# One-core two-block transformer kernel: first norm's gain spread by TensorE, two weight chunks in halves, two key chunks and VectorE's contexts moved

## What is computed

```python
def first_block(x, mem, ...):                       # DEPTH = 2
    mem_n = rmsnorm(mem, mem_norm_gain)
    for l in range(DEPTH):
        h = rmsnorm(x, g[0])
        y = even_mixer(h, ...) if l % 2 == 0 else odd_mixer(h, ...)   # recurrence+pooling | band attention
        x = x + rmsnorm(y, g[1])
        h = rmsnorm(x, g[2])
        x = x + rmsnorm(memory_cross_attention(h, mem_n, w_mem_q[l], w_mem_kv[l], w_mem_o[l]), g[3])
        h = rmsnorm(x, g[4])
        x = x + rmsnorm(squared_relu_mlp(h, w_ff1[l], w_ff2[l]), g[5])
# second block: SwiGLU, stick-breaking attention (layer 0) or sliding window with sinks (layer 1), SwiGLU
```

## Time and profile before

| | |
|---|---|
| median of 3 runs | 1888.31 us |
| profiled execution | 1888.25 us, span 1886.5 us |
| mean granted TensorE clock | 0.994 |
| TensorE busy (matmul) | 1838.3 us, 97% of the span |
| VectorE, ScalarE, GpSimd busy | 54%, 45%, 4% |
| DMA | 318.51 MB, mean 169 GB/s |
| chain that ended last | TensorE 93%, VectorE 3%, ScalarE 2% |

### The profile page before, as it was taken

The page is one execution under the profiler, slowest core; times in us unless marked ns, Lnnn a source line. Parts: engine busy times, 40 slices in busy tenths (PEclk is TensorE's granted clock), DMA queues, the critical chain, the costliest instruction groups (busy, mean ns, idle before and its releaser), DMA issues.

```text
span 1886.5 us, 30104 instructions
## 1 busy us (share of the span) xinstructions
PE 1838.3 (97%) x12718; PEld 1675.1 (89%) x12718; DVE 1022.3 (54%) x1041; ACT 855.2 (45%) x1040; POOL 71.2 (4%) x117
## 2 busy tenths in 40 slices
PE   7999999999999999999999999999999999899998
PEld 6989979999989889998999897899989998779997
DVE  5665454446456464446555544655565555765554
ACT  5535454446555445445333454433343334453333
POOL 1000000000120000000000011000010000110000
PEclk9999999999999999999999999999999999899999
DMA  8616345556556355555555544455555554336552
GB/s 278 205 31 220 129 154 181 186 193 198 162 163 202 104 174 192 185 178 168 181 191 184 161 134 135 148 187 180 193 176 181 192 183 156 112 98 205 187 178 89
DMA packets 224428, 318.51 MB, mean 169 GB/s; under 512 B 5568, under 2 KB 194128, under 8 KB 224352
## 3 DMA queue, kind: packets, MB, share of 16 engines
q1 hardware_dynamic: 219552, 301.48, 48.6%
q0 software_dynamic: 4800, 15.94, 2.7%
HBM read 316.35 MB, written 1.05 MB: 168 GB/s over the span
## 4 chain that ended last, share of the span: by engine, by line
PE 93%; DVE 3%; ACT 2%; issue 1%; DMA 1%; POOL 0%; SPq 0%; DVEq 0%; ACTq 0%
PE C L1429 49%; PE Y L1441 29%; PE Y L1429 7%; DVE xn L1002 1%; ACT xn L631 1%; PE C L1797 1%; PE C L1655 1%; DMA raw<-in_w_in_ab 1%; PE C L1563 1%; PE C L1602 1%; PE Y L1776 1%; PE Y L1610 1%; PE C L1590 0%; PE Y L1580 0%; PE Y L1489 0%
## 5 line engine op out<-in xcount | busy, mean ns | idle before, releaser
L973 DVE TENSOR_TENSOR w_lo<-raw,w_hi 128x2048 fp32r<-128x2048 f32 x284 | 649.5, 2290 | 498.6 <-ACT w_hi L626 498.3
L626 ACT ACTIVATE w_hi<-raw 128x2048 fp32r<-128x2048 f32 x284 | 542.5, 1910 | 371.6 <-PE Y L1441 219.6
L1429 PE MATMUL C<-at_h,w_hi 128*128 128x256 f32 x2160 | 592.0, 284 | 2.6 <-ACT at_h L655 2.6
L1429 PE MATMUL C<-at_h,w_lo 128*128 128x256 f32 x2160 | 590.7, 283 | 0.0
L1429 PE MATMUL C<-at_l,w_hi 128*128 128x256 f32 x2160 | 590.4, 283 | 0.0
L1429 PEld LDWEIGHTS C<-at_h,w_hi 128*128 128x128 f32 x2160 | 405.2, 192 | 7.2 <-issue 4.6
L1429 PEld LDWEIGHTS C<-at_l,w_hi 128*128 128x128 f32 x2160 | 405.3, 192 | 3.0 <-issue 0.5
L1429 PEld LDWEIGHTS C<-at_h,w_lo 128*128 128x128 f32 x2160 | 405.3, 192 | 0.0
L1441 PE MATMUL Y<-w_hi,hid_h 128*128 128x512 f32 x656 | 205.0, 394 | 6.9 <-issue 6.9
L1441 PE MATMUL Y<-w_lo,hid_h 128*128 128x512 f32 x656 | 203.4, 391 | 0.0
L1441 PE MATMUL Y<-w_hi,hid_l 128*128 128x512 f32 x656 | 203.4, 391 | 0.0
(11 more groups left out here) (249 smaller groups left out, 2199.9 us busy)
## 6 DMA issues: line engine op xcount, KB each, us to landing
raw<-in_ffn_w_in SPq DMA_DIRECT2D x88, 1024.0 KB, 5.0
raw<-in_w_ff SPq DMA_DIRECT2D x64, 1024.0 KB, 5.2
raw<-in_ffn_w_out SPq DMA_DIRECT2D x44, 1024.0 KB, 5.0
raw<-in_w_mem_kv SPq DMA_DIRECT2D x16, 1024.0 KB, 5.9
raw<-in_w_qkv SPq DMA_DIRECT2D x12, 1024.0 KB, 5.3
raw<-in_sb_w_qkv SPq DMA_DIRECT2D x12, 1024.0 KB, 5.1
raw<-in_w_in_ab SPq DMA_DIRECT2D x10, 1024.0 KB, 7.9
raw<-in_w_mem_q SPq DMA_DIRECT2D x8, 1024.0 KB, 5.1
```

What stands on the lines that cost most here:

```text
L626: nc.scalar.activation(w_hi[:, n % RING, :], raw[:, n % RAW, :], ACT.Copy).then_inc(hi_split, 1)
L973: V.tensor_tensor(w_lo[:, n % RING, :], raw[:, n % RAW, :], w_hi[:, n % RING, :].bitcast(f32), ALU.subtract).then_inc(lo_split, 1)
L1429: last = mm(to, *passes[k][j], start=step == 0, stop=step == 3 * KT - 1)
```

## The change

Start: the first gain arrives as one row in `first_row`; TensorE spreads it over 128 partitions by two f32 matmuls with a row of ones (`first_ones`, set by GpSimd) into Y banks 0 and 1, ahead of the 20 warm-ups, and VectorE scales from there. The first two weight chunks (`HALVED` = 2) are loaded, split and used in halves of four k-tiles, in an order written out on each engine; the first chunk's result goes to Y bank 2. GpSimd waits until both front halves are rounded before it issues the second gain and all later transfers. Two of layer 1's four key chunks run after the memory attention of layer 0, in a "meanwhile" stage that takes the place of its ("post",) and ("norm", "at"); there the norm's transposes come after both chunks and `clear_y` after the first feed-forward chunk. In layer 1's stage two key chunks are left. In `att` VectorE does the contexts ahead of shares or keeps.

```diff
-                net += [("meanwhile", mem_k(1), mem_k_to), ("att", "band", qkv_cols, "w_o_att"),
+                net += [("meanwhile", mem_k(1)[2:], mem_k_to[2:]), ("att", "band", qkv_cols, "w_o_att"),
...
-            net += [("cols", mem_q(l), q_to), ("softmax", 4), ("rows", "w_mem_o", l),
-                    ("post",), ("norm", "at"), ("relu_ff", l)]
+            net += [("cols", mem_q(l), q_to), ("softmax", 4), ("rows", "w_mem_o", l)]
+            net += [("meanwhile", mem_k(1)[:2], mem_k_to[:2])] if l == 0 else [("post",), ("norm", "at")]
+            net += [("relu_ff", l)]
...
+            def load_halves(src, n):
+
+                to = raw[:, n, :].rearrange("p (k n) -> p k n", k=KT)
+                sp.dma_start(to[:, 0:4, :], src[:, 0:4, :]).then_inc(front_in[n], 16)
+                sp.dma_start(to[:, 4:8, :], src[:, 4:8, :]).then_inc(loaded[n], 16)
+
+            sp.dma_start(first_row, gain_rows[0][None, :]).then_inc(first_gain_in, 16)
             for b in range(TB):
                 sp.dma_start(x[:, b, :], a["x"][0, b * P:(b + 1) * P, :]).then_inc(tokens_in[b], 16)
-            sp.dma_start(gain[:, 0, :], gain_rows[0].partition_broadcast(P)).then_inc(first_gain_in, 16)
...
+            nc.gpsimd.memset(first_ones, 1.0).then_inc(first_ones_set, 1)
             pool.dma_start(ident[:], a["ident"]).then_inc(ident_in, 16)
...
+                if s[0] == "even_cols":
+                    pool.wait_ge(front_hi, HALVED)
...
-                    hi(0)
-                norm_hi(to, at, C)
-                if at.chunk == 0:
-                    for n in range(1, AHEAD):
-                        hi(n)
+                    hi_front(0)
+                    norm_hi(to, at, C, [0])
+                    hi_back(0)
+                    norm_hi(to, at, C, [1])
+                    hi_front(1)
+                    hi_back(1)
...
+                    lo_front(0)
+                    norm_lo(to, at, C, [0])
+                    lo_back(0)
+                    norm_lo(to, at, C, [1])
+                    lo_front(1)
+                    lo_back(1)
...
+                    for k in CONTEXTS_BEHIND.get(j - 1, ()):
+                        contexts(k, at, kind)
                     if p is not None:
                         if kind == "band":
                             shares("band", p, at)
                         else:
                             keeps(p)
-                    for k in CONTEXTS_BEHIND.get(j - 1, ()):
-                        contexts(k, at, kind)
...
+            def col_halves(n, bank, split=None):
+
+
+                wh, wl = (w[:, n, :].rearrange("p (k c) -> p k c", k=KT) for w in (w_hi, w_lo))
+                for i in range(2):
+                    part = slice(i * P, (i + 1) * P)
+                    for step, (half, j) in enumerate(((0, 0), (0, 1), (0, 2), (1, 0), (1, 2), (1, 1))):
...
+                if same:
+                    pe.wait_ge(cols_copied, at.copied)
                 col_chunk(n, "T", at_h, at_l, C[:, 0, :], split=at.turned - 4)
+                if same:
+                    clear_y(at)
...
+                        pe.wait_ge(cols_copied, at.copied + 1)
                         norm(at, Y)
...
+                        pe.wait_ge(first_ones_set, 1)
+                        pe.wait_ge(first_gain_in, 16)
+                        for k in range(2):
+                            gained = mm(Y[:, k, :], first_ones, first_row[:, k * 512:(k + 1) * 512], start=True, stop=True)
+                        gained.then_inc(first_gain_ready, 1)
                         stay_warm(WARM_START)
```

More of the change, by code:

```diff
@@ L231, in build @@
         at_lo = sem("at_lo")
-        first_gain_in = sem("first_gain_in")
+        first_gain_in, first_ones_set, first_gain_ready = sem("first_gain_in"), sem("first_ones_set"), sem("first_gain_ready")
+        front_in = [sem(f"front_in{i}") for i in range(HALVED)]
+        front_hi, front_lo = sem("front_hi"), sem("front_lo")
         gains_in = [sem(f"gains_in{i}") for i in range(2)]
@@ L626, in hi, with hi_front, hi_back @@
                 nc.scalar.activation(w_hi[:, n % RING, :], raw[:, n % RAW, :], ACT.Copy).then_inc(hi_split, 1)
+            def hi_front(n):
+                act.wait_ge(front_in[n], 16)
+                nc.scalar.activation(w_hi[:, n, 0:1024], raw[:, n, 0:1024], ACT.Copy).then_inc(front_hi, 1)
+            def hi_back(n):
+                act.wait_ge(loaded[n], 16)
+                nc.scalar.activation(w_hi[:, n, 1024:2048], raw[:, n, 1024:2048], ACT.Copy).then_inc(hi_split, 1)
             def guess(src, b, at):
@@ L648, in norm_guess, with norm_hi @@
                     guess(mem_x[:, b, :] if to == "mem" else x[:, b, :], b, at)
-            def norm_hi(to, at, banks):
-                for b in range(TB):
+            def norm_hi(to, at, banks, blocks=range(TB)):
+                for b in blocks:
                     for h in range(2):
@@ L687, in copied @@
                 f = ACT.Silu if specs is even_cols and i < 2 else ACT.Copy
-                nc.scalar.activation(to[i], tiles(C[:, i % 4, :], 2), f).then_inc(cols_copied, 1)
+                src = Y[:, 2, :] if specs is even_cols and i == 0 else C[:, i % 4, :]
+                nc.scalar.activation(to[i], tiles(src, 2), f).then_inc(cols_copied, 1)
             def part_copied(i, kind, at):
@@ L700, in meanwhile @@
                 post(at, behind_rows)
-                for i in range(len(specs)):
+                n = len(specs)
+                for i in range(n):
                     hi(at.chunk + i + AHEAD)
-                    if i == len(specs) - 1:
+                    if n > 2 and i == n - 1:
                         norm_hi("at", then, Y)
@@ L707, in meanwhile @@
                         norm_guess("at", then)
+                if n == 2:
+                    norm_hi("at", then, Y)
             def cols(specs, to, at):
@@ L974, in lo, with lo_front, lo_back @@
                                 ALU.subtract).then_inc(lo_split, 1)
+            def lo_front(n):
+                dve.wait_ge(front_hi, n + 1)
+                V.tensor_tensor(w_lo[:, n, 0:1024], raw[:, n, 0:1024], w_hi[:, n, 0:1024].bitcast(f32),
+                                ALU.subtract).then_inc(front_lo, 1)
+            def lo_back(n):
+                dve.wait_ge(hi_split, n + 1)
+                V.tensor_tensor(w_lo[:, n, 1024:2048], raw[:, n, 1024:2048], w_hi[:, n, 1024:2048].bitcast(f32),
+                                ALU.subtract).then_inc(lo_split, 1)
             def newton(guess, mean, scratch):
@@ L998, in scaled @@
                 if at.norm == 0:
-                    dve.wait_ge(first_gain_in, 16)
-                else:
-                    dve.wait_ge(gains_in[at.norm % 2], 16 * ((at.norm + 1) // 2))
+                    dve.wait_ge(first_gain_ready, 1)
+                    return V.scalar_tensor_tensor(xn[:, b, :], src, stat[:, 6, j:j + 1], Y[:, 0:2, :].rearrange(flat), ALU.mult, ALU.mult)
+                dve.wait_ge(gains_in[at.norm % 2], 16 * ((at.norm + 1) // 2))
                 return V.scalar_tensor_tensor(xn[:, b, :], src, stat[:, 6, j:j + 1], gain[:, at.norm % 2, :], ALU.mult, ALU.mult)
@@ L1007, in norm_scale, with norm_lo @@
                     scaled(src, b, at, to == "same").then_inc(xn_ready, 1)
-            def norm_lo(to, at, banks):
+            def norm_lo(to, at, banks, blocks=range(TB)):
                 h, l = (mem_h, mem_l) if to == "mem" else (at_h, at_l)
-                for b in range(TB):
+                for b in blocks:
                     for k in range(2):
@@ L1023, in norm @@
                 if at.chunk == 0:
[L1024 to L1029, removed]
+                    lo_front(0)
[4 more added lines that the diff above has]
+                    lo_back(1)
+                else:
+                    norm_lo(to, at, C)
+                if to == "same":
+                    rope_keys(at)
+                elif at.chunk > 0:
                     lo(at.chunk - 1 + AHEAD)
-                else:
-                    rope_keys(at)
             def post(at, behind_lo=False):
@@ L1430, in col_chunk @@
                 last.then_inc(chunk_done, 1)
+            def col_halves(n, bank, split=None):
[3 more added lines that the diff above has]
+                    for step, (half, j) in enumerate(((0, 0), (0, 1), (0, 2), (1, 0), (1, 2), (1, 1))):
+                        ready = (((front_hi, n + 1), (front_lo, n + 1)), ((hi_split, n + 1), (lo_split, n + 1)))[half][j == 1]
+                        pe.wait_ge(*ready)
+                        if split is not None:
+                            pe.wait_ge(at_lo if j == 2 else at_hi, split + 2 * i + half + 1)
+                        for k in range(4 * half, 4 * half + 4):
+                            still, moving = ((at_h, wh), (at_h, wl), (at_l, wh))[j]
+                            last = mm(bank[:, i * S:(i + 1) * S], still[:, k, part], moving[:, k, :],
+                                      start=step == 0 and k == 0, stop=step == 5 and k == KT - 1)
```

(14 more changed lines are left out.)

9 lines of the change are left out of this document (8 added, 1 removed).

## The result

The changed kernel takes 1877.52 us (median of 4 runs, 1875.51 to 1879.12) against 1888.3 us: ratio 0.9942, 95% interval 0.9925 to 0.9959, so 10.8 us faster, where 15.9 were forecast (1872.4). The mean granted clock rose from 0.994 to 0.996.

The account below looks back on a forecast made before the run. TensorE was taken as the bound, so only its idle or slow-clock stretches could be won. Start -5.2, key chunks -3.6 and VectorE's order -7.1 made -15.9, so 1872.4 us; range 1869.0 to 1879.5.

Parts of the forecast that it names:

- The start: From launch to the end of chunk 1: first chunk at 15.5, chunk 1 done by 27.0, gain 5.2 us.
- The pair: Two f32 gain matmuls ahead of the warm-ups on TensorE's queue: 1.0 to 2.0 us, taken as 1.9.
- The 20 warm-ups: On TensorE behind the gain matmuls: 1.0 us still slow, 3.85 fast, the clock rising 2.9 us after 6.16 again.
- Rival 2: Start gains 0 to 2.6: one-row matmuls don't wake the clock, warm-ups stay slow, or halves late; 1875 to 1878; chance 0.11.
- GpSimd held back: GpSimd waits until about 17.6; VectorE's bounds at 27.1 at worst, chunk 3's split 29.4, wanted 32.8: hidden, 3.4 us spare.
- Key chunks: Two key chunks moved to layer 0: +5.5 us there, -9.1 in layer 1, together -3.6.
- VectorE's order: Contexts first in both attentions: stands shrink by 1.2 and 2.2 us, clock held at both; together -7.1.
- term of 1.84 us for each kept clock: At each attention's shortened stand the clock holds, saving 1.84 us in the row chunk behind; ends 0 and -1.84.
- Rival 3: The attention stands are not the low part's, as the profile names "issue": -7.1 goes, 1879.5; chance 0.04.
- rival 1: Clock falls in the two norm stretches (+3.7) or at the band attention (+1.8): 1874 to 1878; chance 0.24.
- rival 4: TensorE stays at half clock through chunks 0 to 3, costing 23 us: 1895; chance 0.02.
- Rival 5: At the start the first block's data and warm-ups run closer, 1 to 3 us more: 1869 to 1871; chance 0.08.

Follow-up runs that it names:

- e6: Changed kernel with 20 warm-ups first, then the pair of one-row matmuls, then the wait for the identity: 1873.28 us.
- e11: Changed kernel with five more one-row f32 matmuls in place of the 20 warm-ups: 1880.64 us.
- e1: Kernel before with only the change's start (gain spread by TensorE, two chunks in halves, GpSimd held back): 1885.95 us.
- e2: Kernel before with only the two key chunks moved: 1885.74 us.
- e5: Changed kernel with the pair of one-row matmuls ahead of TensorE's wait for the identity, warm-ups still behind it: 1873.39 us.
- e8: Changed kernel without GpSimd's wait for the two front halves: 1877.34 us.
- e4: Changed kernel without one-row matmuls, the first gain coming as a broadcast transfer behind x: 1873.76 us.
- e3: Kernel before with only VectorE's contexts moved ahead of shares and keeps: 1881.63 us.
- e7: Changed kernel with the norm's low parts ahead of the last weight chunk's in the stages of two key chunks: 1874.65 us.
- e12: e10 without GpSimd's wait for the two front halves: 1869.8 us.
- e10: Changed kernel with e7's edit, the gain by a broadcast transfer behind x, and 28 warm-ups ahead of the wait for the identity: 1867.54 us.
- e9: Changed kernel with e7's edit; at the start 14 warm-ups, the one-row pair, 6 warm-ups, then the wait for the identity: 1869.47 us.

## Why the prediction was right, and where it was not

**The start: right in sign, mis-sized by 4.1 us.** Chunk 0 was put at 15.5 and came at 19.64. Three terms make that up.
- The pair: 1.9 us forecast, 3.77 measured. The step that failed is the reading of the earlier trace rows. Its "x4" was taken for four matmuls at 0.49 us; they are two, with two records each. So a pair costs 1.97 at the full clock, as there and as in e6 (1.92), and 3.77 at half. That is 1.9 us.
- The 20 warm-ups: 4.85 us forecast, 6.92 measured. The step that failed is "the clock rises 2.9 us after 6.16 again". It took the pair for work that brings the rise nearer; e11 shows that it does not, and that is 1.0 of the 2.1 (the 20 alone took 5.83). And it took one execution's 2.9 us for a property. In the profiles, from the first warm-up to the change of spacing, it was 2.8 (before), 3.3 (e1), 3.4 (e2), 3.8 (e5), 4.7 (e6, e8), 5.1 (the changed kernel), 5.5 (e4), 5.8 (e3), 5.9 us (e7); in the later ones 2.5 (e12), 3.3 (e10) and over 5 (e9). That is the other 1.1.
- The identity came at 6.54, not 6.16 (0.4); transposes and three warm-ups took 0.2 less.

Rival 2 had the mechanism as its first condition ("the two one-row matmuls do not wake the clock") and its times, 1875 to 1878, hold the result; with 0.11 it had too little. Its third condition, late halves, is not what happened.

A step that the prediction didn't take is the question why the start should wait for TensorE at all. It said that the warm-ups, not the gain, set the transposes, and then weighed only the cost of putting more in front of them. The warm-ups need zeros, not the identity; e6, e9 and e10 start them at 1.44.

**The spread.** The forecast treated the start as one number. Before, the first chunk hung on the weight transfer, and it stood at 19.01, 19.20 and 19.01 in the kernel before, e2 and e3, with rises 2.8, 3.4 and 5.8 us after the warm-ups began. In the changed kernel it hangs on the warm-ups, so each microsecond of a later rise costs half a microsecond. The times of the runs do not settle whether this shows: four of the changed kernel lie within 3.6 us, four of before beside them within 0.9, but 21 of before in a later series within 3.5. The start is not the only place that differs between executions: a clock that falls behind a stand costs 1.5 us in e4's profile and 2.6 in e2's.

**GpSimd held back: right that nothing waits.** VectorE's wait for the bounds ended at 32.01 (forecast 27.1 at worst), since they were issued at 22.5 and not 17.6; the split behind them ended at 34.9 and TensorE wanted it at 36.9. Hidden, with 2 us to spare. That the wait itself buys nothing (e8) the forecast left open.

**Key chunks: right to 0.1 us.** Feed-forward 14.66 us behind the rows' end (14.65), projections 9.0 us earlier (9.1), with VectorE's low parts as the last thing waited for in both, as it was worked out. In layer 1 the profile names the weight split just ahead of them; that the stand is gone in e7, where that split comes later still, says that it was the low parts. What the forecast had in its hands and didn't draw out is the loss in it: the low parts stood behind a split that was not urgent (e7, 2.9 us).

**VectorE's order: right, its clock term not in every execution.** -7.2 in e3 against -7.1. The stands were put at 2.2 and 1.4 us and are 2.18 and 1.36; the chunks behind them take 5.7 us, 0.2 over the 5.47 that was taken. The term of 1.84 us for each kept clock took the old fall and the new hold as fixed. e2's stand of 3.37 us was without a fall and e4's of 2.18 us with one; the count behind e3 says how rare both were. Rival 3 falls: though the profile says "issue", the stand was the low part's.

**Rivals 1 and 4, the clock.** It fell in none of the four places of the changed kernel's profile. In others rival 1 came true in one place each: at the band attention's stand in e4's, in layer 1's norm stretch in e6's. The code at both places is that of the changed kernel, so it differs from execution to execution; how often in one kernel was not measured. Among the 11 profiles with the moved key chunks one of 22 norm stretches was followed by half clock. The Trainium skill (TensorE: Matmul & The Clock Gate, Part 4: PE-mode transpose) would have had it fall in both norm stretches, 1876.1. The total comes near that number by accident: the windows 268 to 272 and 462 to 468 are at 1.00, so the measurement decides against that use of the rule here, e6's one fall notwithstanding. Chunks 0 to 3 ran at 0.12 us spacing from their first matmul, so rival 4 falls too. Rival 5 did not occur.

## What to carry to other kernels

Before an instruction is put on the engine that sets the end, ask which wait stands ahead of it and whether it needs that wait: the same two matmuls cost 3.8 us behind the identity's wait and nothing ahead of it. When a start is shortened, follow who becomes last at each step (transfer, then TensorE's queue, then the gain's scaling, then a weight chunk 25 us behind chunk 1): a hold-back that is worth nothing at one step was worth some 2 us at another. Of consumers on one engine, serve first the one that the bounding engine wants first; in this kernel that was worth 7.2 us in the attentions and 2.9 in the norm stages.

## What the runs showed of the hardware that was not expected

- An f32 matmul of 512 columns leaves two records. Two of them take 1.97 us at full speed; one row on each side makes it no cheaper (1.92 us for two in e6, 3.77 at half speed).
- f32 matmuls of one row did not raise the clock in 12.3 us of unbroken work (e11), where bf16 ones of 128 rows raised it after 2.5 to 5.9 us in the other 13 profiles. The Trainium skill (TensorE: Matmul & The Clock Gate, Part 1) says that the number of slow matmuls at the start of one and the same kernel varies from run to run; the loads at 0.43 us spacing here agree: about 7 in the profile of the kernel before and 14 in e3's, whose start is the same, and from 6 to 14 over all.
- The windows' granted clock reads 1.00 in the first 15 us of the changed kernel, while the spacing there is that of half clock; in e11 it reads 1.00 over transposes that take 1.90 us. At the start of a trace the spacing is to be read, not the column.
- Whether a stand costs the clock is not fixed by its length. One of 3.37 us left it up in e2's profile, one of 2.18 us at the same place was followed by 0.50 in e4's; of the stands of 2.18 and 1.36 us in the other profiles with the new order none was. Norm stretches of 3 to 4 us of transposes with stands of 1.41 and 1.75 us kept it in the changed kernel's profile; in e6's the one in layer 1 did not.
- The one-row pair, 1.55 us of standing and the transposes behind it were followed by 0.50 (e6); with six warm-ups between pair and transposes it stayed at 1.00 (e9). Stands of 0.89 us (e10) and 2.19 us (e12) behind warm-ups, with transposes after them, kept it too.
